# Expert stage of a small diffusion transformer: adding expert results to token rows inside the expert loop

## What is computed

```python
def moe_swiglu(t, w_router, w1, w3, w2):
    logits = (t @ w_router).astype(jnp.float32)
    top_v, top_i = lax.top_k(logits, TOP_K)
    gates = jax.nn.softmax(top_v, axis=-1).astype(t.dtype)
    ...
    h = jax.nn.silu(lax.ragged_dot(xs, w1, sizes)) * lax.ragged_dot(xs, w3, sizes)
    y = lax.ragged_dot(h, w2, sizes) * gates.reshape(-1)[order][:, None]
    return jnp.zeros_like(t).at[tok].add(y)
...
x = x + ga_f[:, None, :] * rmsnorm(channel_mixer(hx), g_ffn_post[i])
```

## Time and profile before

| | us |
|---|---|
| median of 3 runs (lowest, highest) | 8565.12 (8563.59, 8566.45) |
| profiled execution, its own time | 8564.82 |
| its span, first to last instruction | 8563.0 |
| TensorE busy | 8155.6 |
| VectorE / ScalarE / GpSimd busy | 4091.4 / 1458.9 / 4179.8 |

### The profile page before, as it was taken

The page is one execution under the profiler, slowest core; times in us unless marked ns, Lnnn a source line. Parts: engine busy times, 40 slices in busy tenths (PEclk is TensorE's granted clock), DMA queues, the critical chain, the costliest instruction groups (busy, mean ns, idle before and its releaser), DMA issues. The chain is left out here.

```text
span 8563.0 us, 124934 instructions
## 1 busy us (share of the span) xinstructions
PE 8155.6 (95%) x43578; PEld 6030.7 (70%) x43578; DVE 4091.4 (48%) x8936; ACT 1458.9 (17%) x3708; POOL 4179.8 (49%) x4049
## 2 busy tenths in 40 slices
PE   8987999899999999897999999999999999999994
PEld 5575666547777777545787777777777777777773
DVE  3345455434454545644555554455455444444444
ACT  1134322221010101132122111011011011011002
POOL 0010667605666665313666665555555555544434
PEclk9998999999999999998999999999999999999997
DMA  7443788834565653225666665655655555554435
GB/s 262 157 142 121 260 299 296 302 116 165 201 216 216 220 206 113 84 93 194 221 226 233 229 220 196 211 208 196 210 203 206 179 193 178 192 184 161 153 124 222
DMA packets 787887, 1671.81 MB, mean 195 GB/s; under 512 B 38504, under 2 KB 546840, under 8 KB 740972
## 3 DMA queue, kind: packets, MB, share of 16 engines
q1 hardware_dynamic: 731858, 1458.44, 48.4%
q0 software_dynamic: 55584, 207.41, 6.4%
HBM read 1299.49 MB, written 364.13 MB: 194 GB/s over the span
## 5 line engine op out<-in xcount | busy, mean ns | idle before, releaser
L3163 PE MATMUL ex_ps<-ex_xt,land_rows 128*128 x6272 | 958.0, 296 | 31.9 <-issue 31.9
L3163 PEld LDWEIGHTS ex_ps<-ex_xt,land_rows 128*128 128x128 f32 x6272 | 862.5, 191 | 140.2 <-issue 140.2
L3163 PE MATMUL ex_ps<-ex_tx,land_rows 128*128 x6272 | 941.4, 293 | 16.7 <-DVE ex_tmp L3413 16.7
L3466 DVE TENSOR_TENSOR ex_ym<-ex_ps,ex_ym 128x512 f32<-128x512 f32 x1176 | 811.4, 690 | 238.9 <-PE ex_ps L3219 238.9
L3069 POOL TENSOR_TENSOR ex_sa<-ex_a 128x128 f32<-128x128 f32 x182 | 82.7, 454 | 1657.4 <-DVE ex_a L3405 1657.4
L3163 PE MATMUL ex_ps<-ex_tx,ex_sm 128*128 x6272 | 880.8, 294 | 3.4 <-DVE ex_tx L3368 3.4
L3163 PEld LDWEIGHTS ex_ps<-ex_tx,land_rows 128*128 128x128 f32 x6272 | 855.7, 191 | 25.4 <-DVE ex_tmp L3413 22.2
L3163 PEld LDWEIGHTS ex_ps<-ex_tx,ex_sm 128*128 128x128 f32 x6272 | 841.7, 192 | 3.6 <-issue 3.6
L3219 PE MATMUL ex_ps<-land_rows,ex_a 128*128 128x512 f32 x1680 | 784.2, 593 | 0.1
L3054 POOL TENSOR_TENSOR ex_sm<-land_rows 128x512 f32<-128x512 f32 x394 | 501.0, 1272 | 137.1 <-PE ex_ps L3163 114.6
L3278 ACT ACTIVATE ex_tmp<-ex_ps 128x144 f32<-128x144 f32 (+4 forms) x392 | 116.0, 296 | 2503.5 <-PE ex_ps L3163 2503.1
(11 more groups left out here) (470 smaller groups left out, 13469.3 us busy)
## 6 DMA issues: line engine op xcount, KB each, us to landing
land_rows<-in_o_w SPq DMA_DIRECT2D x593, 1024.0 KB, 5.0
land_rows<-wt SPq DMA_DIRECT2D x197, 1024.0 KB, 7.0
ma_cqT<-in_o_w SPq DMA_DIRECT2D x112, 1024.0 KB, 7.3
wt<-ma_bt SPq DMA_DIRECT2D x112, 1024.0 KB, 5.1
de_wr<-in_e_w SPq DMA_DIRECT2D x88, 1024.0 KB, 5.6
xs<-de_zero POOLq DMA_DIRECT2D x136, 512.0 KB, 7.0
ys<-de_zero POOLq DMA_DIRECT2D x136, 512.0 KB, 8.1
en_ch<-in_w_mod SPq DMA_DIRECT2D x48, 1024.0 KB, 5.6
```

Source lines behind the costliest of these rows:

```text
L3163: last = nc.tensor.matmul(PS[:, bank, 0:h], left[:, k], right[k], start=start and k == 0, stop=k == HK - 1, skip_group_check=not start)
L3466: nc.vector.tensor_tensor(out, new, out, ALU.add).then_inc(y_added[t], 1)
```

## The change

Each expert row gets a record of 16 words in a DRAM table: the row of z that it adds to, at three widths, the place of its gate, and the token that is finished with it. fourier scatters these records beside the rows (32 more indirect DMAs of GpSimd) after one copy that fills the table with defaults. ys is gone; z (2048 token rows and 512 spare ones) takes its place, and is what dense clears (20 blocks instead of 136).

At the end of a job GpSimd gathers the gates of the job's rows (`gather_gates`, four indirect DMAs), ScalarE multiplies YO by them, GpSimd multiplies YA, and GpSimd adds the rows to z by four indirect DMAs that accumulate (`add_rows`). In the job that follows, the 512 rows from the first row of the job before are finished in four tiles: GpSimd gathers z (`gather`), ScalarE squares and roots (`roots`, after chunks 2 and 9) and scales (`norms`, after chunks 3 and 10), VectorE inverts, GpSimd multiplies by the gate vector and adds x by an accumulating indirect DMA (`scale`, in chunks 4, 5, 11, 12), and scatters to out (`store`, in chunks 6, 7, 12, 13). The finish stage does the last job's 512 rows alone, with no overlap between its four stores. GpSimd's and ScalarE's chunk loops are written out in part or in full. YA has one buffer instead of two, so VectorE's first add of a job waits until the adds to z of the job before have landed. TensorE, ScalarE, VectorE and GpSimd begin experts only when the gate vector G is loaded as well; its load stands in SyncE's queue behind the first six weight loads.

```diff
-                        pool.dma_start(rows(c, t), ZERO[:, :]).then_inc(cleared, 16)
-            pool.wait_ge(cleared, 16 * n_clear * len(clear))
+                        if t < c.shape[0] // P:
+                            pool.dma_start(rows(c, t), ZERO[:, :]).then_inc(cleared, 16)
+            pool.wait_ge(cleared, 16 * sum(c.shape[0] // P for c in clear))
...
+            sp.dma_start(tab_d, blank_d).then_inc(blank_set, 16)
+            sp.dma_start(NAMES[:, :, :, :], names_d).then_inc(names_in, 16)
...
+                        pool.indirect_dma_start(out=tab_d, out_offset=bass.IndirectOffsetOnAxis(ap=POS[:, k, i:i + 1], axis=0),
+                                                in_=NAMES[:, i, k], in_offset=None).then_inc(named, 16)
...
+            for t in range(TILES):
+                pool.indirect_dma_start(out=Z[:, t], out_offset=None, in_=z_d,
+                                        in_offset=bass.IndirectOffsetOnAxis(ap=LAST[:, t, 0:1], axis=0)).then_inc(z_in[t], 16)
+            for t in range(TILES):
+                pool.indirect_dma_start(out=X[:, t], out_offset=None, in_=x_d,
+                                        in_offset=bass.IndirectOffsetOnAxis(ap=LAST[:, t, 0:1], axis=0)).then_inc(x_in[t], 16)
+            for t in range(TILES):
                 pool.wait_ge(summed, t + 1)
-                pool.indirect_dma_start(out=out, out_offset=bass.IndirectOffsetOnAxis(ap=ORD[:, t:t + 1], axis=0),
-                                        in_=X(t), in_offset=None).then_inc(stored[t % DEPTH], 16)
-                if t + DEPTH < NT:
-                    gather(t + DEPTH)
-            for s in range(DEPTH):
-                pool.wait_ge(stored[s], 16 * len(range(s, NT, DEPTH)))
+                if t:
+                    pool.wait_ge(stored, 16 * t)
+                pool.indirect_dma_start(out=out, out_offset=bass.IndirectOffsetOnAxis(ap=LAST[:, t, 1:2], axis=0),
+                                        in_=X[:, t], in_offset=None).then_inc(stored, 16)
+            pool.wait_ge(stored, 16 * TILES)
...
+            sp.dma_start(G[:, :], gate.rearrange("(a n) -> a n", a=1).to_broadcast([P, D])).then_inc(const_in, 16)
+            sp.dma_start(LAST[:, :, :], table[ROWS_END:ROWS_END + BANK, 14:16].rearrange("(t p) w -> p t w", p=P)).then_inc(last_in, 16)
+            sp.dma_start(share_d[SEQ:SEQ + BANK], no_share_d).then_inc(shares_in, 16)
+            sp.wait_ge(share_made, 1)
+            sp.dma_start(share_d[0:SEQ].rearrange("(t p) k -> p t k", p=P), GK[:, :, :]).then_inc(shares_in, 16)
...
                     sp.wait_ge(stored, j * 64 + 64)
                     sp.sem_inc(y_free, 1)
+
+                    def names(r0, n):
+                        return table[bass.ds(sp.snap((row + r0).with_bounds(min_val=0, max_val=ROWS_END + r0)), n)]
+
+                    sp.dma_start(IX[:, 0:2], names(0, 2 * P)[:, 0:6].rearrange("(r p) w -> p r w", p=P)).then_inc(ix_in, 16)
...
+                    sp.wait_ge(o_stored[0], j * 32 + 32)
+                    sp.sem_inc(passed_sp, 1)
+                    sp.wait_ge(o_stored[1], j * 32 + 32)
+                    sp.sem_inc(passed_sp, 1)
+                    sp.dma_start(LAST[:, :, :], names(0, BANK)[:, 14:16].rearrange("(t p) w -> p t w", p=P)).then_inc(last_in, 16)
...
+            def gather(j, tile):
+                s = tile % 2
+                if tile == 0:
+                    pool.wait_ge(last_in, j * 16 + 16)
+                    pool.sem_inc(passed_pool, 1)
+                    pool.wait_ge(stored, j * 64 + 64)
+                    pool.sem_inc(passed_pool, 1)
+                if tile >= 2:
+                    pool.wait_ge(o_stored[s], j * 32 + 16)
+                    pool.sem_inc(passed_pool, 1)
+                pool.indirect_dma_start(out=Z[:, s], out_offset=None, in_=z_d,
+                                        in_offset=bass.IndirectOffsetOnAxis(ap=LAST[:, tile, 0:1], axis=0)).then_inc(z_in[s], 16)
+
+            def scale(j, tile):
+                s = tile % 2
+                pool.wait_ge(normed, j * 4 + (tile + 1))
+                nc.gpsimd.tensor_tensor(Z[:, s], Z[:, s], G[:, :], ALU.mult).then_inc(scaled, 1)
+                pool.wait_ge(scaled, j * 4 + (tile + 1))
+                pool.sem_inc(passed_pool, 1)
+                pool.indirect_dma_start(out=Z[:, s], out_offset=None, in_=x_d, in_offset=bass.IndirectOffsetOnAxis(ap=LAST[:, tile, 0:1], axis=0),
+                                        compute_op=ALU.add).then_inc(x_added[s], 16)
+
+            def store(j, tile):
+                s = tile % 2
+                pool.wait_ge(x_added[s], j * 32 + 16 * (tile // 2 + 1))
+                pool.sem_inc(passed_pool, 1)
+                if tile:
+                    pool.wait_ge(o_stored[1 - s], j * 32 + 16 * ((tile - 1) // 2 + 1))
+                    pool.sem_inc(passed_pool, 1)
+                pool.indirect_dma_start(out=out, out_offset=bass.IndirectOffsetOnAxis(ap=LAST[:, tile, 1:2], axis=0),
+                                        in_=Z[:, s], in_offset=None).then_inc(o_stored[s], 16)
+
+            def gather_gates(j, h):
+                pool.wait_ge(ix_in, j * (16 * 7) + 16 * 7)
+                pool.sem_inc(passed_pool, 1)
+                pool.wait_ge(shares_in, 32)
+                for s in range(4):
+                    of = s if s < len(pieces(h)) else 0
+                    pool.indirect_dma_start(out=GT[:, s:s + 1], out_offset=None, in_=share_d.rearrange("r (k a) -> (r k) a", a=1),
+                                            in_offset=bass.IndirectOffsetOnAxis(ap=IX[:, of, 1:2], axis=0)).then_inc(gates_in, 16)
+
+            def add_rows(i, j, t, h):
...
+                for s, part in parts:
+                    place, width = part[5], part[4] * (2 if part[0] == 1 else 1)
+                    nc.gpsimd.tensor_scalar(YA[:, place:place + width], YA[:, place:place + width], GT[:, s:s + 1], None, ALU.mult).then_inc(part_weighed, 1)
+                if len(parts) < 2:
+                    pool.sem_inc(part_weighed, 2 - len(parts))
...
+                for r in range(2):
+                    pool.wait_ge(weighed, j * 2 + (r + 1))
+                    pool.sem_inc(passed_pool, 1)
+                    if r in whole:
+                        for c in range(2):
+                            pool.indirect_dma_start(out=z_d.rearrange("r (g n) -> (r g) n", g=2),
+                                                    out_offset=bass.IndirectOffsetOnAxis(ap=IX[:, r, 2 + 2 * c:3 + 2 * c], axis=0),
+                                                    in_=YO[:, r, c], in_offset=None, compute_op=ALU.add).then_inc(stored, 16)
+                    else:
+                        pool.indirect_dma_start(out=z_d, out_offset=bass.IndirectOffsetOnAxis(ap=IX[:, r, 0:1], axis=0),
+                                                in_=YO[:, r].rearrange("p c n -> p (c n)"), in_offset=None, compute_op=ALU.add).then_inc(stored, 16)
...
+            pool.wait_ge(const_in, 48)
+            for q in range(4):
+                pool.dma_start((GT[:, 0:2], GT[:, 2:4], ss[:, 0, 0:2], ss[:, 0, 2:4])[q], no_share_d[0:P]).then_inc(stored, 16)
...
+                    for f in range(FC):
                         step(f, 1 - f % 2, j * (FC // 2) + (f + 1) // 2)
+                        if f == 1:
+                            gather(j, 0)
+                            gather(j, 1)
+                        if f in (4, 5, FC - 3, FC - 2):
+                            scale(j, {4: 0, 5: 1, FC - 3: 2, FC - 2: 3}[f])
+                        if f in (6, 7, FC - 2, FC - 1):
+                            store(j, {6: 0, 7: 1, FC - 2: 2, FC - 1: 3}[f])
+                        if f in (7, 8):
+                            gather(j, f - 5)
+                        if f == FC - 2:
+                            gather_gates(j, h)
+                    add_rows(i, j, t, h)
...
+                    if x == 0:
+                        pe.wait_ge(squared, j * 4)
...
+                    def roots(pair):
+                        for s in range(2):
+                            tile = 2 * pair + s
+                            act.wait_ge(z_in[s], j * 32 + 16 * (pair + 1))
+                            if tile:
+                                act.wait_ge(squared, j * 4 + tile)
+                            act.sem_inc(passed_act, 1)
+                            nc.scalar.activation(XT[:, bass.ds(other, 1), HK:HK + 2, :].rearrange("p a k n -> p (a k n)"), Z[:, s], ACT.Square,
+                                                 accum_out=ss[:, 0, tile:tile + 1]).then_inc(squared, 1)
+                        act.wait_ge(squared, j * 4 + (2 * pair + 2))
+                        nc.scalar.activation(ss[:, 1, 2 * pair:2 * pair + 2], ss[:, 0, 2 * pair:2 * pair + 2], ACT.Sqrt, bias=eps[:, 0:1],
+                                             scale=1.0 / D).then_inc(rooted, 1)
+                        nc.scalar.activation(warm[:, :], eps[:, :], ACT.Silu)
+
+                    def norms(pair):
```

(24 more changed lines are left out.)

220 lines of the change are left out of this document (118 added, 102 removed).

## The result

The changed kernel takes 8666.74 us (median of 4 runs, 8660.8 to 8669.19) where the kernel before takes 8564.35 (4 runs, 8561.37 to 8566.45): 1.0119 times as long, with a 95% interval of 1.0107 to 1.0131. The forecast was 8565, with a range up to 8612. The change makes the kernel slower by 102 us, and the cause lies in the job loop.

A forecast was written before the change was run, and what follows sets the result against it. TensorE was taken to bound experts, something else the tail, with GpSimd lacking slack in h = 128 jobs. Terms -65 - 16 + 0 + 19 + 4 + 33.5 + 8 + 5 + 12 = +0.5 gave 8565 us, range 8520 to 8612.

The forecast's parts named there:

- tail: End of the program after experts: 120.6 us before, four store periods after; gain 65 us.
- table loads (32 passes): ScalarE's chunk loop in h = 128 jobs: 32 passes without the load before `keep`, 0.5 each, gain 16 us (11 to 19).
- start of experts: TensorE's start in experts waits for G behind weight loads: everything moves by 19 us (8 to 24).
- fourier: Last two tiles of fourier have four scatters more, the last starting 5 us later: 4 us (0 to 6).
- boundaries on GpSimd, with fetch and clock: Job boundaries: late GpSimd stalls TensorE 33.5 us, code fetch of the jump back 8, lower clock after stalls 5.
- SyncE held by `stored`: After a boundary, SyncE's wait for the adds delays chunk 2's W1: 0, up to 4 us per h = 128 boundary.
- ScalarE: Job loop: `roots` stalls 2 us in all, `norms` in chunk 10 makes `keep` late, 10 us; sum 12 (3 to 25).
- The step that failed first: Chunk 12 of GpSimd's queue: multiply, x add, store and gate gathers take 10.2 us, making recombine 4.7 or 4.4 late.
- 1.25 us for an issue: Indirect DMAs on GpSimd at job boundaries: 1.25 us each; last store and four adds 6.25 us.
- rival 2: Indirect issues at boundaries cost more than 1.25 us; half taking 0.8 more gives +48, 8613 us; chance 0.23.
- Rival 3: Switching tables drains ScalarE, `roots` 2.8 us longer in the h = 128 jobs: +16, 8581 us; chance 0.10.
- Rival 1: GpSimd and ScalarE hide most of the boundary work; a third of 58.5 us of stalls stays: 8526 us; chance 0.27.

The follow-up runs named there:

- e1: Changed kernel with SyncE issuing W1 and W3 of chunk 2 before its wait for the adds to z: 8632.96 us.
- e4: Changed kernel with the load of G on its own semaphore, awaited only by GpSimd's first multiply by it: 8644.32 us.
- e2: Changed kernel with multiply and x add of tiles 2 and 3 moved from chunks 11 and 12 to 9 and 10: 8575.91 us.
- e-kernels: The follow-up kernels, each the changed kernel with one or more edits; measured from 8510.29 to 8646.40 us.
- b1: Kernel before, plus one unread indirect gather per job on GpSimd, ahead of chunk 12's weight sums: 8574.69 us against 8562.86.
- e7: Changed kernel with the x add and the adds to z in experts as plain copies, so its output differs: 8596.59 us.
- e10: Changed kernel with e1, e2 and e4, gate gathers in chunk 8, stores of tiles 2 and 3 in idle stretches of chunks 10 and 11: 8510.29 us.

## Why the prediction was wrong

From the trace, in us (parts of the span; the measured ones sum to 101.4, and the span grew by 101.7):

| step | forecast | measured |
|---|---|---|
| tail | -65 | -62.3 |
| table loads (32 passes) | -16 | -19 |
| start of experts | +19 | +20 |
| fourier | +4 | +9.9 |
| boundaries on GpSimd, with fetch and clock | +46.5 | +72.1 (chunks 13, 0; some 10 of it is held VectorE) |
| SyncE held by `stored` | 0 | +29 (what e1 takes off chunks 1 and 2) |
| rest of chunks 1 to 3, mostly the clock behind the wait in chunk 0 | 0 | +14 (the tables' gain taken out) |
| VectorE held in chunk 12 | 0 | +36.4 (chunk 12) |
| ScalarE | +12 | +4.2 |
| stages ahead of fourier | 0 | -2.9 |

**The tail** came out as forecast, with errors that partly cancel: 1.3 us between adds became 1.9, the barrier took longer, and the stores came 5.1 and twice 4.1 us apart. **The start of experts** was right, and e4 shows it: G's load landed last, later than I had it (TensorE started at 4010.25), in a stage that itself began 7 us later. **Table loads** gave 0.6 us a pass. **ScalarE** was mis-sized: `roots` never cost anything visible, and `norms` only 0.6 us in an h = 128 job; e2, where it moves to chunk 9, leaves nothing of it (0.0).

**The step that failed first** is the price of the multiply and the x add in the second half of a job. The sum has the pair in chunk 12 of GpSimd's queue ("Chunk 12 gets ...: 10.2 us") only by how late it makes recombine, and the pair in chunk 11 not at all. It took GpSimd's idle time as cover and left out what VectorE was doing in that stretch. Measured, VectorE's token sums are held, 36.4 us in TensorE's chunk 12 and some 10 more in chunk 13. Six e-kernels move or cut that work, and chunk 12 follows each time: 36.4 with multiply and x add there, 22.0 without the multiply, 13.6 with the multiply in quarters, 13.7 with a store in place of both, 3.2 or 2.5 with nothing beside the token sums; b1 makes 14.3 us out of one issue in the kernel before. The trace of the kernel before held a sign of it, in VectorE's timeline of the same chunk:

```profile
4500.91 0.38 DVE L3351 TENSOR_TENSOR ex_tx<-ex_xt  x1
...
4501.81 0.86 DVE L3351 TENSOR_TENSOR ex_tx<-ex_xt  x1
```

The second sum takes twice the first, and GpSimd is in a weight sum then (4500.95 to 4502.43). The forecast read GpSimd's and TensorE's timelines there, not VectorE's. The Trainium skill, "SBUF — State Buffer", section Who interferes with whom, says that a VectorE instruction with two inputs in SBUF contends with a GpSimd instruction that reads SBUF, that the port pair they share is an exclusive lock, and that the order of issue decides who blocks. The traces agree: 0.38 us alone, 1.94 beside the 2.59 us multiply, 0.38 again beside its quarters, with the quarters stretched from 2.79 to 3.67 us. This rule spoke against the change, and the forecast didn't weigh it.

**The second** is "I reckon that W1 lands just when it is needed ...: 0, but up to 4 us for each h = 128 boundary". Chunk 1 is 3.6 to 4.7 us longer in three h = 128 jobs, chunks 1 and 2 together 1.7 to 6.8 in those of 144, 43 us in all with the tables' gain taken out, and 29 of them are late weights. The last add is issued 26.6 us after the start of recombine (4575.66 to 4602.25), sooner than the 31 I wrote, but SyncE goes on only 11.0 us later, and W1, issued 28 us after the p6, is not there for another 10. I had set no number for either. The mechanism stood in the text as what could make the forecast wrong; its price of 0 had no row behind it. e1 (-29 in chunks 1 and 2) shows it, and e7 (-39, with GpSimd earlier too) agrees. The other 14 us are mostly TensorE at a lower clock behind the wait before: the forecast had 5 us for that, at three boundaries.

**The third** is a size, 1.25 us for an issue: rival 2's point. Accumulating ones take 1.57 + 0.30 between two. Recombine, too, starts 6.0 us later than before in the h = 128 jobs and mostly 5.5 in those of 144, where I had 4.7 and 4.4. So for h = 144 the third sum for chunk 1 ends 52.0 us after the p6 of chunk 13 (44.3 before) where my sum puts it at 48.3, and TensorE, due at 48.0, is 4.1 us late in place of the 0.4 I worked out. For h = 128 the forecast was 7.6 us at that point; it is 11.0. Rival 2 named the right side and part of the cause, but its 8613 lacks the held VectorE, and its late weights have no price. Rival 3 falls: ScalarE showed no drain worth 2 us. Rival 1 falls as well for this order of the work, though e10 comes out below its 8526.

**Fourier** remains half open: the last scatter starts 392.6 us into the stage, 383.7 before. Of this 5.0 are the four more scatters forecast. The other 3.9 are not steady: the e-kernels don't touch this stage, and their last scatter starts 388.1 to 392.7 us into it. What moves it no experiment tested.

## What to carry to other kernels

Idle time of an engine covers new work only if the engines beside it do nothing that shares a port with it: before putting GpSimd work into a gap, read VectorE's timeline over the same microseconds for operations whose inputs are all in SBUF, and put the work where there are none. For an indirect DMA read also what stands behind it in GpSimd's queue: here it held VectorE only with a computation directly behind it. The same work in other places of the same queues, with G's load on a semaphore of its own, turned +102 us into -53. A wait put into a queue that loads weights has to be priced by the next load behind it, with the time at which that load was issued before and the landing time of what is waited for; if no row has that landing time, the range must hold it.

## What the runs showed of the hardware that I had not expected

- An indirect DMA that accumulates takes 1.54 to 1.66 us to issue on GpSimd and 7.9 to 11.8 us from the last issue until the waiting queue goes on; the same DMA without the addition 0.97 and 3.2 to 8.7. The length of the issue hardly depends on the record: 1.59 us for 128 rows of 1024 elements, 1.57 for 128 of 512.
- A VectorE operation between SBUF buffers that starts 0.35 us or more into an indirect DMA's issue stands still until the computation directly behind the issue in GpSimd's queue has ended: 1.88 us instead of 0.38 beside an issue of 0.99 and the sum behind it (b1). With another indirect DMA behind the issue it is free: 0.38 us at most in 57 cases (changed kernel).
- GpSimd's multiply of 128x1024 takes 2.59 us beside VectorE's token sums in one piece and 3.67 in four (2.79 in four without them), and a token sum beside it 1.94 and 0.38 us.
- TensorE pays for a wait again afterwards. Windows of the changed kernel behind two waits of TensorE at a boundary, columns as in the earlier trace rows:

```profile
4588.90:4594.20 5.30, 5.30 (x25) 5.30 (x26) 0.58 (x2) 0.67 (x1) 5.07 (x5) 0.50 0.00 0
4607.90:4612.30 4.40, 4.40 (x25) 4.40 (x26) 0.58 (x2) 0.00 (x0) 4.17 (x6) 0.61 0.90 266
```

The granted clock is 0.50 over 5.3 us behind waits of 1.99 and 2.29 us close together, which is the level of 1.2 GHz, and 0.61 over 4.4 us behind one of 3.29. So some 2.7 and 1.7 us of work were lost on top of the waits, where the forecast had 1.7 for a boundary of h = 128.
